# Top-k positions in PSUM, gate products in half steps over three banks, and more row dots inside the gate steps

## The chip, the cores and the metric

The kernel runs on one core of one Trainium2 chip. The metric is the device time of one execution in microseconds; the median of three runs is compared. The engines are called as in the profile: PE (TensorE), DVE (VectorE), ACT (ScalarE), POOL (GpSimd), SP (SyncE, which only issues DMAs here).

## What is computed

The program is a transformer block of two layers for 512 tokens of width 1024. The change touches only the PEER feed-forward of the first layer: each token picks, per head, 16 of 16,384 single-neuron experts.

```
q = (xb @ wq).reshape(PEER_BLOCK, PEER_HEADS, 2, PEER_HALF)
s = einsum('thpd,hpkd->thpk', q, sub_keys)
s_top, i_top = lax.top_k(s, PEER_TOPK)
cand_s = s_top[:, :, 0, :, None] + s_top[:, :, 1, None, :]
cand_i = i_top[:, :, 0, :, None] * PEER_N_KEYS + i_top[:, :, 1, None, :]
best_s, best_pos = lax.top_k(cand_s, PEER_TOPK)
experts = take_along_axis(cand_i, best_pos, axis=-1)
g = softmax(best_s)
act = gelu(einsum('thkd,td->thk', expert_u[experts], xb))
out = einsum('thk,thkd->td', g * act, expert_v[experts])
```

## The kernel before

**Two ways through the experts.** For three of the four blocks of 128 tokens (384 tokens, `TD = 3`) the kernel computes all experts densely: 128 "U tiles" (one tile is 128 experts: 24 matmuls of 384 columns, with each weight split into a high and a low part, `whi` and `wlo`), and later 128 "V tiles". The gates of these tokens are scattered into a dense array by "gate steps". For the last block of 128 tokens each token's own 128 expert rows are fetched instead: an indirect DMA on POOL's queue (`fetch_u`, 128 rows of 4 KB, one for each partition, 512 KB in all) brings one expert row per token into a ring of four buffers `UROW`, and a DVE instruction (`dot`) multiplies it with the token's row and sums. There are 128 such dots. Row k may be fetched once dot k-4 is done.

**The order of the work** is written out by hand, engine by engine, with semaphores between. On DVE it is: the top-k of the scores (`lists_top`), the four `topk` blocks (in the order token block 3, 0, 1, 2; the last three carry 6, 11 and 11 dots between their instructions), 96 gate steps, the tail of the U tiles, and the V tiles.

**U tiles.** For each, SP loads the raw weights, ACT rounds them to `whi` (line 777), POOL (line 641) or, for the last tiles, DVE (line 2301) computes `wlo`, PE multiplies (lines 1275 to 1277), and ACT applies gelu into `actb` (line 982) and stores it. There are four buffers each. 36 tiles run beside the top-k. PE then waits for the normalised gates (`gsel`, line 2247), transposes them, and runs four more tiles.

**Gate steps.** Step q handles four tokens. POOL subtracts indices (`OJ`, shown as T, line 708), DVE makes one-hot matrices `OI` (line 2271) and `OG` (line 2275), PE multiplies them, four matmuls of 256 columns into one pair of PSUM banks (line 1596), ACT copies the high half to `GS` (line 1018), and DVE adds the low half (line 2285). Banks 4 and 5 serve the even steps, 6 and 7 the odd ones. Before each group of four PE does five eighths of a U tile, so 60 tiles (`GATE_TILES`) lie in the 96 steps. Bank 3 holds `window`, the indices and gates of 32 steps. Banks 2 and 3 hold `x_row`, the rows of the last token block, until then; ACT has copied them to SBUF as `sc_row` (shown as rr), and dots from number 28 on read that copy.

**The tail** is the 28 U tiles after the gate steps: PE does nothing else, DVE makes their `wlo` and two dots after each of 25 tiles, and SP stores the last of the dense gates. Then come the **V tiles**, in which DVE makes the products, their low parts, `wlo`, an addition of one fetched V row, and a dot in every tile that `V_DOT_TILES` lists.

In `topk` the found positions `bp` are split into a row and a column (`bab`, then `babf` as float), corrected in a few small instructions, and compared with `iota` to pick the indices.

Of the kernel before, what the change touches and what calls it, by code (L numbers as in the profile page):

```python
# [19 lines left out]
U32 = mybir.dt.uint32  # L20
# [6 lines left out]
P = 128  # L27
# [41 lines left out]
GATE_TILES = 60  # L69
# [42 lines left out]
def build(nc, A, out):  # L112
    with ExitStack() as ctx:
# [111 lines left out]
        bab = a2("bab", [P, 2, NH, 16], U32)  # L225
        babf = a2("babf", [P, 2, NH, 16])
# [410 lines left out]
        def _(pool):  # L637
# [133 lines left out]
        def _(act):  # L771
# [239 lines left out]
            def g_group(q, m, stored=None):  # L1011

                act.wait_ge(g_done, q + 1)
                if stored is not None:
                    act.wait_ge(g_out[m // 16], stored)
                t = 4 * (m % 16)
                high = pair[m % 2][:, :, :].rearrange("p b (t w j) -> p w j (b t)", t=2, w=2)[:, 0]
                nc.scalar.activation(GS[:, m // 16, :, t:t + 4], high, ACT.Copy).then_inc(g_high, 1)

            def gate_blocks(i, first):  # L1020

                for n in range(32):
                    u = 5 * n // 8
                    if n == 0 or 8 * u // 5 == n or -(-8 * u // 5) == n:
                        ahead(G0["U"], u % 4, i * 5 + (GATE_IT + u // 4))
                    if n >= 2:
                        g_group(i * 32 + (n - 2), n - 2, i * 64 if (n - 2) % 16 == 0 and not first else None)
                    elif not first:
                        g_group(i * 32 + (n - 2), n + 30)
                    if 8 * u + 7 < 5 * n + 5:  # L1030
                        it = i * 5 + (GATE_IT + u // 4)
                        act_tile(it * 4 + u % 4, u % 4, it * 32 + 16 * (u % 4 // 2))

            gate_blocks(0, True)
            with act.Fori(1, TD) as i:
                gate_blocks(i, False)
            for m in (30, 31):
                g_group(32 * (TD - 1) + m, m)
# [233 lines left out]
        def _(pe):  # L1272
# [316 lines left out]
            def gate_group(q, half, peeled=False):  # L1589
# [13 lines left out]
            def gate_step(i, n):  # L1603

                for unit in range(5 * n, 5 * n + 5):
# [1138 lines left out]
```

## Time and profile before

| | us |
|---|---|
| median of three runs | 2507.83 (2507.5 to 2508.65) |
| profiled execution, its own time | 2507.04 |
| span of the profiled execution | 2505.2 |
| PE busy | 2414.8 (96% of the span) |
| DVE busy | 1558.9 (62%) |
| POOL busy | 1238.3 (49%) |
| ACT busy | 938.6 (37%) |

The span runs from the first to the last instruction; the execution's own time has 1.84 us more around it. The mean granted clock of PE is 0.991.

### The profile page before, as it was taken

To read this page: it belongs to the slowest core of one execution; us is meant where nothing else is said; L and a number is where in the kernel's file an instruction comes from. 1 tells how busy PE (TensorE), PEld (TensorE's weight loads), DVE (VectorE), ACT (ScalarE), POOL (GpSimd) and SP (SyncE) were. 2 spreads that over 40 slices of the span, in tenths; PEclk is the share of its full clock that TensorE was granted. 3 is DMA by queue.
4 is the path that set the end of the run, shared out by engine and by line. 5 is a ranking of instruction groups with operands and counts; after the bars stand their busy time and mean duration, and the time that the engine had idled before them with its cause. 6 is when DMAs were issued, how large, how long until landed. Compare 5 with 4: busy or idle time off the path is not lost.

```text
span 2505.2 us, 36450 instructions
## 1 busy us (share of the span) xinstructions
PE 2414.8 (96%) x12832; PEld 2165.7 (86%) x12832; DVE 1558.9 (62%) x2682; ACT 938.6 (37%) x1394; POOL 1238.3 (49%) x676
## 2 busy tenths in 40 slices
PE   7999998999889999898999999999999999999998
PEld 4878886899889999888999999998867888888887
DVE  5268333899968888677999899886256414422201
ACT  4473333333434444333333333333344323332222
POOL 3305443348768888554555454544402544444443
PEclk9999999999999999999999999999999999999999
DMA  7228433248856777899999999993301333333332
GB/s 274 75 110 286 154 93 126 85 122 270 281 163 226 246 270 232 333 370 362 394 395 395 389 394 376 392 335 103 100 26 50 116 95 99 87 94 98 101 94 75
DMA packets 254500, 518.83 MB, mean 207 GB/s; under 512 B 117760, under 2 KB 150912, under 8 KB 250048
## 3 DMA queue, kind: packets, MB, share of 16 engines
q1 hardware_dynamic: 197552, 350.01, 42.9%
q0 software_dynamic: 38416, 142.36, 14.6%
q10 hardware_dynamic: 18432, 25.17, 2.7%
q8 instruction: 56, 0.92, 0.2%
q14 instruction: 44, 0.36, 0.0%
HBM read 462.95 MB, written 54.53 MB: 207 GB/s over the span
## 4 chain that ended last, share of the span: by engine, by line
PE 66%; DVE 14%; DMA 12%; issue 4%; SPq 3%; ACT 1%; POOL 1%; ACTq 0%; DVEq 0%; POOLq 0%
PE bank L1275 16%; PE bank L1277 16%; PE bank L1276 16%; DMA GJ<-gate_dram 7%; DMA X<-in_u_rows,which 4%; PE pair L1277 3%; PE pair L1275 3%; PE pair L1276 3%; DVE X L2163 2%; PE pair L1596 2%; DVE YROW L2359 2%; SPq L510 1%; DVE wlo L2301 1%; DVE T L2228 1%; SPq L594 1%
## 5 line engine op out<-in xcount | busy, mean ns | idle before, releaser
L641 POOL TENSOR_TENSOR wlo<-wraw,whi 128x1024 fp32r<-128x1024 f32 x303 | 743.1, 2456 | 802.7 <-ACT whi L777 801.8
L1275 PE MATMUL bank<-HH,whi 128*128 128x512 f32 (+1 forms) x2048 | 752.7, 368 | 36.1 <-DVE wlo L2301 12.1
L1276 PE MATMUL bank<-HL,whi 128*128 128x512 f32 (+1 forms) x2048 | 745.5, 364 | 0.0
L1277 PE MATMUL bank<-HH,wlo 128*128 128x512 f32 (+1 forms) x2048 | 745.2, 364 | 0.0
L777 ACT ACTIVATE whi<-wraw 128x1024 fp32r<-128x1024 f32 x456 | 481.4, 1057 | 519.1 <-PE bank L1277 214.2
L1275 PEld LDWEIGHTS bank<-HH,whi 128*128 128x128 f32 x2048 | 388.0, 189 | 87.4 <-issue 25.2
L1277 PEld LDWEIGHTS bank<-HH,wlo 128*128 128x128 f32 x2048 | 387.3, 189 | 40.5
L1276 PEld LDWEIGHTS bank<-HL,whi 128*128 128x128 f32 x2048 | 388.0, 189 | 39.4 <-issue 0.5
L701 POOL DMA_INDIRECT VROW<-in_w,which x128 | 214.2, 1673 | 255.2 <-DVE YROW L2359 242.3
L694 POOL DMA_INDIRECT X<-in_u_rows,which x128 | 165.5, 1293 | 100.0 <-DVE dots L2163 73.9
L2301 DVE TENSOR_TENSOR wlo<-wraw,whi 128x1024 fp32r<-128x1024 f32 x153 | 186.3, 1218 | 1.3 <-ACT whi L777 1.3
L1275 PE MATMUL bank<-WH,whi 128*128 128x384 f32 x512 | 172.8, 337 | 3.4 <-DVE WL L2334 3.3
L1275 PE MATMUL pair<-WH,whi 128*128 128x384 f32 x512 | 171.6, 335 | 0.0
L1277 PE MATMUL bank<-WH,wlo 128*128 128x384 f32 x512 | 171.3, 335 | 0.0
L1276 PE MATMUL pair<-WL,whi 128*128 128x384 f32 x512 | 171.3, 335 | 0.0
L1276 PE MATMUL bank<-WL,whi 128*128 128x384 f32 x512 | 171.3, 334 | 0.0
L1277 PE MATMUL pair<-WH,wlo 128*128 128x384 f32 x512 | 171.2, 334 | 0.0
L2359 DVE SCALAR_TENSOR_TENSOR YROW<-VROW,wexp,YROW 128x1024 f32<-128x1024 f32 x128 | 166.0, 1297 | 0.2
L1045 ACT ACTIVATE WH<-AJ 128x384 fp32r<-128x384 f32 x128 | 67.1, 524 | 240.7 <-DVE AJ L2328 240.6
L2163 DVE CUSTOM_DVE_ANT_0 X<-X,rr 128x1024 f32<-128x1024 f32 x100 | 131.3, 1314 | 41.6 <-DMA X<-in_u_rows,which 41.6
L2396 DVE TENSOR_TENSOR T<-bank,rr 128x512 f32<-128x512 f32 x60 | 41.3, 690 | 177.1 <-PE bank L1277 176.9
L982 ACT ACTIVATE actb<-bank 128x384 f32<-128x384 f32 x128 | 63.0, 492 | 213.2 <-PE bank L1277 204.6
(409 smaller groups left out, 3737.3 us busy)
## 6 DMA issues: line engine op xcount, KB each, us to landing
wraw<-in_w SPq DMA_DIRECT2D x456, 512.0 KB, 4.2
act_dram<-actb ACTq DMA_DIRECT2D x128, 192.0 KB
gate_dram<-GS SPq DMA_DIRECT2D x24, 1024.0 KB, 8.3
AJ<-act_dram SPq DMA_DIRECT2D x128, 192.0 KB, 7.1
GJ<-gate_dram SPq DMA_DIRECT2D x128, 192.0 KB, 9.0
adaw<-in_ada SPq DMA_DIRECT2D x32, 512.0 KB, 5.6
ada<-in_ada SPq DMA_DIRECT2D x16, 512.0 KB, 14.2
NB<-in_nab POOLq DMA_DIRECT2D x4, 1024.0 KB, 5.7
```

Source lines behind the costliest of these rows:

```text
L641: nc.gpsimd.tensor_tensor(wlo[:, slot, :, :].rearrange("p k c -> p (k c)"), wraw[:, slot, :, :].rearrange("p k c -> p (k c)"), whi[:, slot ...
L694: pool.indirect_dma_start(UROW[:, k % R, :], None, A["u_rows"], bass.IndirectOffsetOnAxis(which[:, 0, k:k + 1], 0)).then_inc(u_row[k % R], 16)
L701: pool.indirect_dma_start(VROW[:, k % R, :], None, A["w"].rearrange("g p c -> (g p) c"), bass.IndirectOffsetOnAxis(which[:, 1, k:k + 1], 0 ...
L777: nc.scalar.activation(whi[:, slot, :, :].rearrange("p k c -> p (k c)"), wraw[:, slot, :, :].rearrange("p k c -> p (k c)"), ACT.Copy).then ...
L982: nc.scalar.activation(actb[:, u % 2, :], bank[u % 2][:, 0:SD], ACT.Gelu_apprx_tanh).then_inc(tile_evac, 1)
L1045: nc.scalar.activation(WH[:, slot, :], AJ[:, slot, :], ACT.Copy).then_inc(pw_hi, 1)
L1275: pe.matmul(out_, ah, bh, start=first, stop=False, **kw)
L1276: pe.matmul(out_, ah, bl, start=False, stop=False, **kw)
L1277: return pe.matmul(out_, al, bh, start=False, stop=last, **kw)
L2163: nc.vector.tensor_tensor_reduce(UROW[:, n % R, :], UROW[:, n % R, :], x_row if n < TOP_DOTS else sc_row, 1.0, 0.0, ALU.mult, ALU.add, dot ...
L2301: nc.vector.tensor_tensor(wlo[:, slot, :, :].rearrange("p k c -> p (k c)"), wraw[:, slot, :, :].rearrange("p k c -> p (k c)"), whi[:, slot ...
L2359: nc.vector.scalar_tensor_tensor(YROW[:, :], VROW[:, u, :], wexp[:, u:u + 1], YROW[:, :], ALU.mult, ALU.add)\
```

## The change

Four things change. (1) `bab`, `babf` and one of the scratch tiles (`wide`) move from SBUF to PSUM banks 6 and 7, and the conversion of the positions becomes two instructions. (2) The gate steps produce, copy and add in half steps of two tokens, over banks 4, 5 and 6 in turn; bank 7 now holds the window, so banks 2 and 3 keep `x_row`. (3) 64 U tiles instead of 60 lie in the gate steps, 16 eighths to three steps, and 24 dots (every fourth step, reading `x_row` from PSUM) instead of 8. (4) 34 dots instead of 54 lie in the tail, now of 24 tiles, of which DVE makes 21 `wlo`; 42 instead of 38 dots lie in the V tiles. The loops over gate steps on PE and ACT are written out.

```diff
-GATE_TILES = 60
+GATE_TILES = 64
-GATE_DOTS = 8
-U_DOTS = 90
-V_DOT_TILES = [j for j in range(P) if j % 5 in (1, 3)][:P - U_DOTS]
-ACTS = (72, 109, P)
+PSUM_DOTS = TOP_DOTS + STEPS // 4
+U_DOTS = 86
+V_DOT_TILES = [j for j in range(P) if j % 16 in (1, 3, 5, 8, 10, 12, 14)][:P - U_DOTS]
+ACTS = (60, 105, P)
...
+        bab = bank[6][:, 256:512].bitcast(U32).rearrange("p (w h k) -> p w h k", w=2, h=NH)
+        babf = bank[7][:, 0:256].rearrange("p (w h k) -> p w h k", w=2, h=NH)
+        wide = bank[7][:, 256:384].rearrange("p (h k) -> p h k", h=NH)
+        gate_window = bank[7]
...
-                if 8 * (lows - gate0 - 3) // 5 + 1 == q:
+                if 3 * (lows - gate0 - 3) // 2 + 1 == q:
                     lo(G0["U"] + lows, lows % R)
                     lows += 1
-                if q >= 16 and q % 12 == 4:
+                if q >= 8 and q % 4 == 0:
                     fetch_u(fetched)
...
+            def gate_group(q):
+
                 pe.wait_ge(og_ready, q + 1)
-                if not peeled:
-                    pe.wait_ge(g_evac, q - 1)
-                for e in range(4):
-                    t = 4 * half + e
-                    mm = pe.matmul(bank[4 + 2 * half + e // 2][:, e % 2 * 256:e % 2 * 256 + 256], OI[:, t, :],
-                                   OG[:, half, :, e, :], start=True, stop=True)
-                mm.then_inc(g_done, 1)
+                for h in (2 * q, 2 * q + 1):
+                    if h >= 3:
+                        pe.wait_ge(g_evac, h - 2)
+                    for t in range(2):
+                        e = 2 * (h % 2) + t
+                        mm = pe.matmul(bank[4 + h % 3][:, t * 256:t * 256 + 256], OI[:, 4 * (q % 2) + e, :],
+                                       OG[:, q % 2, :, e, :], start=True, stop=True)
+                    mm.then_inc(g_done, 1)
...
-                then(nc.vector.tensor_copy(babf[:, :, :, :], bab[:, :, :, :]))
-                row, place, beyond, wide = babf[:, 0, :, :], babf[:, 1, :, :], last[:, 0, :, :], last[:, 1, :, :]
+                place, beyond, row = last[:, 0, :, :], last[:, 1, :, :], babf[:, 0, :, :]
+                nc.vector.tensor_copy(row, bab[:, 0, :, :])
+                then(nc.vector.tensor_copy(place, bab[:, 1, :, :]))
...
             for q in range(STEPS):
                 if q % 32 == 0:
                     window(q // 32)
-                onehots(q)
+                indices_hot(q)
                 if q >= 2:
-                    g_sum(q - 2)
-                if q % 12 == 11:
+                    gate_sum(2 * q - 4)
+                    gate_sum(2 * q - 3)
+                gates_hot(q)
+                if q % 4 == 3:
                     dot()
...
-            for k in range(4):
-                dot()
             v.wait_ge(w_lo, G0["U"] + U_POOL)
+            tail_dots = U_DOTS - PSUM_DOTS
             for t in range(U_POOL, P):
                 lo(G0["U"] + t, t % R)
-                for k in range(2):
-                    if dotted[0] < U_DOTS:
-                        dot()
+                while dotted[0] < PSUM_DOTS + (t - U_POOL + 1) * tail_dots // (P - U_POOL):
+                    dot()
```

**Place 1, a `topk` block on DVE.** `bp`, `gsel`, `last`, `T` and `iota` lie in SBUF; `pair1` is PSUM banks 6 and 7. Before:

```order
L2211 TENSOR_SCALAR bab<-bp 128x128
L2212 TENSOR_SCALAR bab<-bp 128x128
L2213 TENSOR_TENSOR gsel<-bv 128x128
L2216 CAST babf<-bab 128x256
L2218 SCALAR_TENSOR_TENSOR last<-babf 128x128
L2219 TENSOR_SCALAR last<-babf 128x128
L2220 TENSOR_TENSOR last<-last 128x128
L2221 SCALAR_TENSOR_TENSOR babf<-babf,last 128x128
L2222 TENSOR_SCALAR babf<-babf 128x128
L2223 TENSOR_TENSOR babf<-babf,last 128x128
L2228 TENSOR_TENSOR T<-babf,iota 128x2048
```

In the changed kernel, at the same place on DVE:

```order
L2206 TENSOR_SCALAR pair1<-bp 128x128
L2207 TENSOR_SCALAR pair1<-bp 128x128
L2208 TENSOR_TENSOR gsel<-bv 128x128
L2212 CAST pair1<-pair1 128x128
L2213 CAST last<-pair1 128x128
L2214 SCALAR_TENSOR_TENSOR last<-pair1,last 128x128
L2215 TENSOR_SCALAR pair1<-pair1 128x128
L2216 TENSOR_TENSOR pair1<-pair1,last 128x128
L2217 SCALAR_TENSOR_TENSOR pair1<-pair1,last 128x128
L2218 TENSOR_SCALAR pair1<-pair1 128x128
L2219 TENSOR_TENSOR pair1<-last,pair1 128x128
L2224 TENSOR_TENSOR T<-pair1,iota 128x2048
```

Nothing moved but the places of the operands, and one conversion became two; only the instruction that writes `gsel` keeps both inputs in SBUF.

**Place 2, a gate step with a dot on DVE** (`rr` is the SBUF copy of the rows, `bank` in the dot's row is banks 2 and 3). Before:

```order
L2275 SCALAR_TENSOR_TENSOR OG<-T,bank 128x1024
L2285 TENSOR_TENSOR GS<-pair1,GS 128x128x4
L2163 ISA X,dots<-X,rr 128x1024
L2163 ISA dots 128x1
L2271 TENSOR_TENSOR OI<-iota,bank 128x512
```

In the changed kernel:

```order
L2267 TENSOR_TENSOR OI<-iota,pair1 128x512
L2285 TENSOR_TENSOR GS<-pair1,GS 128x128x2
L2285 TENSOR_TENSOR GS<-pair0,GS 128x128x2
L2275 SCALAR_TENSOR_TENSOR OG<-T,pair1 128x1024
L2158 ISA X,dots<-X,bank 128x1024
L2158 ISA dots 128x1
```

The sum stands in two halves, and ahead of `OG` instead of behind it.

**Place 3, the start of the tail on DVE.** Before, after the last sum:

```order
L2285 TENSOR_TENSOR GS<-pair1,GS 128x128x4
L2163 ISA X,dots<-X,rr 128x1024
L2163 ISA dots 128x1
L2163 ISA X,dots<-X,rr 128x1024
L2163 ISA dots 128x1
L2163 ISA X,dots<-X,rr 128x1024
L2163 ISA dots 128x1
L2163 ISA X,dots<-X,rr 128x1024
L2163 ISA dots 128x1
L2301 TENSOR_TENSOR wlo<-wraw,whi 128x1024
```

In the changed kernel:

```order
L2285 TENSOR_TENSOR GS<-pair1,GS 128x128x2
L2303 TENSOR_TENSOR wlo<-wraw,whi 128x1024
L2158 ISA X,dots<-X,rr 128x1024
L2158 ISA dots 128x1
L2303 TENSOR_TENSOR wlo<-wraw,whi 128x1024
L2158 ISA X,dots<-X,rr 128x1024
L2158 ISA dots 128x1
L2158 ISA X,dots<-X,rr 128x1024
L2158 ISA dots 128x1
```

Four dots ahead of the first `wlo` are gone, and a tile is followed by one or two dots.

## Rows read from the trace of the kernel before

**Rows 1.** Waits of PE: place, what for, total us, times, longest.

```profile
PE pair L1582 <- DVE gsel L2247: 17.4, 1, 17.4
PE bank L1275 <- DVE wlo L2301: 12.1, 11, 2.4
PE bank L1275 <- ACT actb L982: 7.1, 2, 6.4
```

**Rows 2.** Windows: us, busy PE, PEld, DVE, ACT, POOL (instructions), PE clock, DMA share, GB/s.

```profile
523.10:677.90 154.80, 151.64 (x866) 151.20 (x865) 152.98 (x452) 66.02 (x83) 114.16 (x61) 0.99 0.76 248
716.80:1011.70 294.90, 294.63 (x1815) 293.60 (x1814) 249.49 (x306) 143.07 (x214) 252.23 (x162) 1.00 0.70 231
1011.70:1157.50 145.80, 126.38 (x673) 121.01 (x672) 102.15 (x149) 44.96 (x60) 78.17 (x59) 0.95 1.00 374
1157.50:1556.00 398.50, 395.14 (x2266) 392.09 (x2265) 353.06 (x472) 144.76 (x190) 200.60 (x127) 1.00 1.06 385
```

**Rows 3.** Timeline of ACT: start, length, the end of two U tiles.

```profile
607.41 0.49 ACT L982 ACTIVATE actb<-bank 128x384 f32<-128x384 f32 x1 [2.13 <-PE bank L1277]
611.57 0.49 ACT L982 ACTIVATE actb<-bank 128x384 f32<-128x384 f32 x1 [2.13 <-PE bank L1277]
```

**Rows 4.** DVE by line, 534.5 to 695.5: count, busy us, mean ns, idle before.

```profile
L2228 DVE TENSOR_TENSOR T<-babf,iota 128x2048 f32<-128x2048 f32 x8 | 20.3, 2541 | 0.2
L2211 DVE TENSOR_SCALAR bab<-bp 128x128 uint32<-128x128 uint32 x4 | 8.8, 2188 | 0.1
L2205 DVE TENSOR_TENSOR T<-T 128x128 f32<-128x128 f32 x4 | 6.6, 1647 | 0.0
L2220 DVE TENSOR_TENSOR last<-last 128x128 f32<-128x128 f32 x4 | 5.4, 1360 | 0.1
L2216 DVE CAST babf<-bab 128x256 f32<-128x256 uint32 x4 | 4.1, 1016 | 0.1
L2213 DVE TENSOR_TENSOR gsel<-bv 128x128 f32<-128x128 f32 x4 | 3.4, 848 | 0.0
L2223 DVE TENSOR_TENSOR babf<-babf,last 128x128 f32<-128x128 f32 x4 | 3.3, 836 | 0.0
```

**Rows 5.** Timeline of DVE in one `topk` block, and of POOL beside it.

```profile
573.94 5.35 DVE L2211 TENSOR_SCALAR bab<-bp 128x128 uint32<-128x128 uint32 x1
...
579.35 0.28 DVE L2213 TENSOR_TENSOR gsel<-bv 128x128 f32<-128x128 f32 x1
579.66 0.29 DVE L2216 CAST babf<-bab 128x256 f32<-128x256 uint32 x1
...
628.85 2.29 DVE L2228 TENSOR_TENSOR T<-babf,iota 128x2048 f32<-128x2048 f32 x1
...
569.84 9.36 POOL L641 TENSOR_TENSOR wlo<-wraw,whi 128x1024 fp32r<-128x1024 f32 x4
```

**Rows 6.** A row fetch on POOL, its dot on DVE, and landing times of rows, 600 to 670.

```profile
655.58 0.95 POOL L694 DMA_INDIRECT X<-in_u_rows,which  x1 [0.16 <-issue]
...
664.28 1.19 DVE L2163 CUSTOM_DVE_ANT_0 X<-X,bank 128x1024 f32<-128x1024 f32 x1
...
DMA to landing us min/median/max: 5.3/6.2/7.3
```

**Rows 7.** Gate steps, 720 to 1011: groups by line.

```profile
L2285 DVE TENSOR_TENSOR GS<-pair,GS 128x512 f32<-128x512 f32 x94 | 64.2, 684 | 3.1 <-ACT GS L1018 3.1
L777 ACT ACTIVATE whi<-wraw 128x1024 fp32r<-128x1024 f32 x59 | 62.7, 1063 | 36.1 <-ACT actb L982 35.0 <-issue 1.1
L1018 ACT ACTIVATE GS<-pair 128x512 f32<-128x512 f32 x94 | 55.4, 590 | 54.6 <-PE pair L1596 54.5
L2163 DVE CUSTOM_DVE_ANT_0 X<-X,rr 128x1024 f32<-128x1024 f32 x8 | 19.1, 2389 | 0.0
```

**Rows 8.** Tail, 1011.7 to 1157.5: the dots by line, and the fetches' median us to landing.

```profile
L2163 DVE CUSTOM_DVE_ANT_0 X<-X,rr 128x1024 f32<-128x1024 f32 x55 | 67.1, 1223 | 41.6 <-DMA X<-in_u_rows,which 41.6
...
X<-in_u_rows,which POOLq DMA_INDIRECT x55, 7.9
```

More of the change, by code:

```diff
@@ L583, in store_g @@
                              GS[:, b % 2, j, :].rearrange("p j t -> p (j t)")).then_inc(g_out[b % 2], 16)
+            stored_at = [-(-32 * (b + 1) // 3) + 6 for b in range(2 * TD)]
             for n in range(GATE_TILES + TAIL):
                 load_w(gu0 + n, (gu0 + n) % R)
-                if n >= 17 and n % 10 in (7, 8, 9, 0) and (n - 17) // 10 < 2 * TD:
-                    store_g((n - 17) // 10, (n - 17) % 10)
+                for b in range(2 * TD):
+                    if 0 <= n - stored_at[b] < 4:
+                        store_g(b, n - stored_at[b])
             def load_ag(j, slot, peeled=False):
@@ L1009, in _, with gate_high @@
                 act_tile(m, u, 16 * (m // 2))
-            def g_group(q, m, stored=None):
-                act.wait_ge(g_done, q + 1)
+            def gate_high(h, stored=None):
+                act.wait_ge(g_done, h + 1)
                 if stored is not None:
[L1015 to L1038, printed above, removed]
+                    act.wait_ge(g_out[h // 32 % 2], stored)
+                t = 2 * (h % 32)
+                high = bank[4 + h % 3].rearrange("p (t w j) -> p w j t", t=2, w=2)[:, 0]
+                nc.scalar.activation(GS[:, h // 32 % 2, :, t:t + 2], high, ACT.Copy).then_inc(g_high, 1)
+            def gate_tile(u):
+                m = 4 * GATE_IT + u
+                act_tile(m, u % 4, 16 * (m // 2))
@@ new lines, in _ @@
+            for n in range(STEPS + 2):
+                v_, part = n // 3, n % 3
+                if part == 0 and n < STEPS:
+                    ahead(G0["U"], 4 * GATE_IT + 2 * v_)
+                for h in range(2 * n - 4, 2 * n - 2):
+                    if h >= 0:
+                        gate_high(h, 64 * (h // 64) if h % 32 == 0 and h >= 64 else None)
+                if part == 1 and n < STEPS:
+                    gate_tile(2 * v_)
+                    ahead(G0["U"], 4 * GATE_IT + 2 * v_ + 1)
+                if part == 2 and n < STEPS:
+                    gate_tile(2 * v_ + 1)
@@ L1587, in _ @@
                 u_tile(G0["U"] + 4 * LEAD_IT + u, u)
[L1589 removed]
+            def gate_group(q):
                 pe.wait_ge(og_ready, q + 1)
[L1592 to L1598 removed]
+                for h in (2 * q, 2 * q + 1):
[6 more added lines that the diff above has]
+                    mm.then_inc(g_done, 1)
             gu0 = G0["U"] + 4 * GATE_IT
             pe.wait_ge(gt_split, 1)
[L1603 to L1605 removed]
+            for n in range(STEPS):
+                for unit in range(16 * n // 3, 16 * (n + 1) // 3):
                     u = unit // 8
[L1607 to L1610 removed]
+                    u_blocks(gu0 + u, u % R, (unit % 8,))
                 if n:
[L1612 to L1617 removed]
+                    gate_group(n - 1)
+            gate_group(STEPS - 1)
             with pe.Fori(0, TAIL // 4) as i:
@@ L2222, in topk @@
                 nc.vector.tensor_scalar(row, row, -1.0, None, ALU.add)
-                then(nc.vector.tensor_tensor(place, place, wide, ALU.add))
+                then(nc.vector.tensor_tensor(babf[:, 1, :, :], place, wide, ALU.add))
                 idx = tkf.rearrange("p (h w) a -> p w h a", w=2)
@@ L2289, in _ @@
                     window(q // 32)
-                onehots(q)
+                indices_hot(q)
                 if q >= 2:
-                    g_sum(q - 2)
-                if q % 12 == 11:
+                    gate_sum(2 * q - 4)
+                    gate_sum(2 * q - 3)
+                gates_hot(q)
+                if q % 4 == 3:
                     dot()
-            for q in range(STEPS - 2, STEPS):
-                g_sum(q)
+            for h in range(2 * STEPS - 4, 2 * STEPS):
+                gate_sum(h)
             def lo(g, slot):
```

41 lines of the change are left out of this document (16 added, 25 removed).

## The prediction

> **What bounds the kernel now.** I read the waits of PE first, since PE is the engine that is busy nearly always, then windows by stage, then the timelines of the engine that PE waits for. In the stages that the change touches PE is idle in two places. It stands 17.4 us before its transposes until DVE has the gates [rows 1]; DVE is busy 153.0 of 154.8 us there [rows 2], so DVE's chain of top-k instructions sets that end. And it waits in the tail, 12.1 us for DVE's `wlo` and 7.1 us for `actb` [rows 1]. A U tile takes 4.16 us (611.57 - 607.41) [rows 3], so 28 need 116.5 us where the tail took 145.8 [rows 2]: 29.3 us are lost. DVE waits there 41.6 us for fetched rows [rows 8] and the DMA share is 1.00 [rows 2]. The gate steps (294.6 of 294.9 us busy) and most of the V stage (395.1 of 398.5) are bound by PE itself [rows 2].
>
> **Top-k: what the move to PSUM removes.** Several small DVE instructions have lengths far over their work. The shift `bab<-bp` took 5.35 us at 573.94; it ended at 579.3, and POOL's run of four `wlo` was 569.84 to 579.20 [rows 5]. The conversion took 0.29 us undisturbed [rows 5] and 1.02 on average [rows 4]. So DVE instructions stand until a POOL instruction lets go. Which ones do is told by the dots: with the row in SBUF, beside the data in SBUF, a dot takes 2.39 us on average [rows 7], with the row in PSUM 1.19 [rows 6].
>
> Excess over undisturbed length for the instructions that lose an SBUF operand [rows 4, 5]: line 2211 8.8 - 4 x 0.22 = 7.9; 2220 5.4 - 4 x 0.28 = 4.3; 2216 4.1 - 4 x 0.29 = 2.9; 2223 3.3 - 1.1 = 2.2; 2228 20.3 - 8 x 2.29 = 2.0. (For the undisturbed shift I take 0.22, a little under the 0.28 of 2213; with 0.28 the sum is 0.2 less.) Sum 19.3 us, on a chain that ends in PE's wait. Two things stop it from all arriving:
> - 2213 (`gsel`, excess 3.4 - 1.1 = 2.3 now) and 2205 (6.6 - 1.1 = 5.5) keep two SBUF inputs. In block two 2213 stands right behind the 5.35 us; with 2211 free it meets the same POOL run. That run begins with the row offsets of block one, which come some 2.4 us earlier (one stand of 2220 and a bit of 2228), so about 2.5 of those 5.1 us are gained, not all. In block four I charge 0.7.
> - The dots inside the blocks need rows, and POOL fetches one after each `wlo`, at the tiles' pace of 4.16 us. Row 21 was fetched at 655.58 and used at 664.28; landing takes 6.2 [rows 6], so it had 2.5 us of slack. POOL itself gets earlier by 2.4 (above) and by some 2 (the 2.3 us comparisons of 2228 no longer hold it), so up to dot 21 the gain is at most about 6.8. What is saved behind dot 21 (2.7 of 2211, 2.9 of 2216, less 0.7) is 4.9 more.
>
> I charge 0.3 us for the extra conversion and slower access in that last part, and less before it, under the cap. Gain 6.8 + 4.9 - 0.3 = 11.4, taken as **11**. Bounds: 3 (nearly every stand passes on to 2213 and 2205) and 17.4 (the whole wait of PE). There is a rule against this edit in the Trainium skill ("VectorE: DVE Perf Modes", Why PSUM operands drop a tier): a PSUM operand costs a float instruction its double rate. By it some six instructions of 128 elements would be about 0.07 us longer in each block, 1.7 us in all, an estimate from that page; the gain would be 10.
>
> **Gate steps: length.** A step now has 16 matmuls of 384 columns instead of 15: 4.16/24 = 0.173 us. 96 steps cost 16.6 us more and the tail has 4 x 4.16 = 16.6 less: zero, if PE stays the bound. Does it? Busy time over 294.9 us now and over 311.5 after:
> - DVE 249.5 [rows 2]. Out: 8 dots, 19.1, and the sums, 64.2 [rows 7]. In: 192 half sums; the length lies between 0.28 (128 elements, rows 5) and 0.684 (512, rows 7), in proportion 0.42 us, so 80; and 24 dots of 1.2 (the one of rows 6 reads PSUM: 1.19), 29. Sum 275, 88%. The dots in gate steps now take 2.39 us on average against 1.2, for both inputs are in SBUF; from PSUM they don't.
> - POOL 252.2 [rows 2] + 4 `wlo` of 2.34 [rows 5] + 15 fetches of 0.95 [rows 6] = 276, 89%.
> - ACT 143.1 + 192 x 0.40 (from 0.59 for 512 elements and 0.49 for 384 [rows 3, 7]) - 55.4 + 8 = 172, 55%.
>
> The order matters more than the shares. The second half of a group waits for a bank that is free when DVE has added the first half of the group before. From the end of a group PE has 15 to 18 matmuls to do, 2.6 us or more. Beside them ACT does, one step in three, `whi` first (1.06), then two halves (0.8), and DVE the one-hot (0.68) and the half sum (0.42): at the worst 2.3 us. After a dot step DVE starts up to 1.2 late, but then `OI` overlaps what ACT does and the sum is there at about 2.5. Hidden, with 0.1 to 1.5 us to spare, where the old order had over 2. I take 0 for the stage. If the cover goes, it is 96 times what is missing.
>
> POOL queues a fetch behind a `wlo` and ahead of the next `OJ`, so each fetch makes an `OJ` 1 us later. POOL runs up to four steps ahead, and has 1 us in 3.2 free on two steps of three: DVE should not see it.
>
> **Tail.** Rows fetched in it fall from 55 to 36 (54 of 90 are fetched before). Megabytes: rows 36 x 0.524 = 18.9; V rows 4 x 0.524 = 2.1; raw weights some 23 x 0.524 = 12.3; `actb` 24 x 0.197 = 4.7; gate stores 4.2; first V operands 1.6: sum 43.8, where before it was 374 GB/s x 145.8 us = 54.5. At 374 GB/s this would be 117 us; the V stage holds 385 over 400 us [rows 2], 114. PE needs 24 x 4.16 = 100. The old 374 was in part set by the ring: four rows in flight and 7.9 us to landing [rows 8] allow one dot in 2.0 us, and with waits it was 145.8/54 = 2.7. DVE now needs 34 dots, at 2.7 92 us, and has 21 tiles (87 us) and the lead that it begins with, up to 3 tiles. So DVE about keeps up, and PE's wait for `wlo` (12.1) nearly goes; the passage to the V stage, where ACT stands for V's weights and PE for `actb` (7.1), I halve. Between 100 and 117 I take 109: 100 + 4 + 5 for the 1 MB stores. Against 145.8 - 16.6 = 129.2 the **tail gives 20** (12 to 27).
>
> **V stage.** Four more dots and rows (2.1 MB). DVE has 353 of 398 us busy; 4 x 1.2 are hidden. The DMA share is 1.06 at 385 GB/s: if that is the ceiling, 2.1/0.385 = 5.5 us come back, if not, 0. PE loses only 3.4 us there now, so I take 1.
>
> **Sum.** -11 + 0 - 20 + 1 = -30 against the profiled execution's span of 2505.2 and own time of 2507.04: span 2475, own time 2477. The median of the runs shown (2507.83) is 0.8 us over that time, so the forecast is **2478**.
>
> **Rivals.**
> - *The stands in the top-k only change place* (chance 0.14): gain 3 instead of 11, 2487. For it: 2213 and 2205 already stand 7.8 us. Against it: POOL is busy 114 of 155 us, so a stand is a matter of chance for each of the eight instructions left. The Trainium skill has this rival as a rule ("SBUF — State Buffer", Who interferes with whom): two inputs in SBUF are enough for a DVE instruction and a GpSimd instruction that reads SBUF to shut each other out for their whole length, and whichever starts first holds. Rows 5 agree, as far as 2211 and POOL's run go.
> - *The tail is bound by its bytes* (0.15): 117 us, gain 12, 2487. For it: share 1.00. Against it: the V stage moves more at 1.06. With the rival above it would be 2495 (0.03 of the two).
> - *The half-step handshake becomes the bound* (0.06): slower. DVE's first half sum would come after PE's 2.6 us. It decides from 30/96 = 0.31 us of waiting a step on; at 0.5 us it is 48, and the result 2508 - 30 + 48 = 2526. For it: the spare time in a dot step is about 0.1 us. Against it: DVE has 12% free to catch up, so the delay doesn't add up.
> - *Nothing comes of it* (0.03): the row fetches hold the top-k at its old pace and bytes the tail, 2508.
> - *As forecast* (0.62): its own range 2470 to 2490.
>
> **Range and chances.** 2478 is the likeliest. The range, 2468 to 2497, holds the forecast with its bounds (-17.4 in the top-k and -27 in the tail, both at once, would give 2465) and both middle rivals, also together. A difference under 0.2% (5 us) can't be told from none. Faster 0.90, same 0.03, slower 0.07.
>
> **What would show it.** Top-k: the PSUM instructions at 0.2 to 0.3 us, the wait for `gsel` near 6 to 9 us, and new waits of DVE for rows inside the blocks. Gate steps: 311 us, PE without idle time, dots at 1.2 us each. Tail: near 109 us, wait for `wlo` under 4 us. V stage: as long as before, its GB/s a little over 385. Wrong it would be by a step of over 3.3 us in the gate steps, by a tail at 117, or by 2213 taking over the 5 us stand in every block.

## The result, and the profile after

The changed kernel takes 2479.98 us (median of four runs, 2478.29 to 2481.64), the kernel before on the same chip 2508.24 (2507.5 to 2509.91). The ratio is 0.9892 (0.9880 to 0.9904): 28 us faster. The forecast was 2478. The profiled execution after took 2481.35 us, its span is 2479.5.

The span falls by 25.7 us. I split it at four events that both traces have: the start of PE's transposes of the gates, the start of its last gate matmul, the end of the U tiles and the end of the V tiles. Four tiles moved from the tail into the gate steps, so in the last column 4 x 4.16 = 16.6 us are taken off the gate steps and added to the tail.

| event or stretch | before | after | difference, tiles set off |
|---|---|---|---|
| transposes start | 695.53 | 684.65 | -10.9 |
| to the last gate matmul | 315.8 | 337.7 | +5.3 |
| to the end of U | 146.1 | 105.0 | -24.5 |
| V tiles | 542.0 | 544.7 | +2.7 |
| rest, second layer | 805.7 | 807.5 | +1.8 |

The waits of PE after, from 480 to 1700 us (what it waited for; us in total, times, longest), to be set against [rows 1]:

```profile
PE pair L1584 <- DVE gsel L2243: 9.9, 1, 9.9
PE bank L1277 <- DVE WL L2334: 4.8, 9, 1.1
PE bank L1277 <- ACT actb L986: 2.9, 1, 2.9
PE pair L1599 <- DVE GS L2285: 2.0, 2, 1.2
```

The wait for `gsel` fell from 17.4, the one for `wlo` in the tail (12.1) is gone, the one for `actb` fell from 7.1. New are two waits for half sums.

The windows after (length, busy PE, PEld, DVE, ACT, POOL, then clock, DMA share, GB/s): gate steps, tail, and the first 399 us of V, against the last three of [rows 2].

```profile
706.80:1022.40 315.60, 312.81 (x1908) 310.75 (x1907) 268.67 (x436) 161.49 (x318) 271.45 (x183) 1.00 0.73 251
1022.40:1127.30 104.90, 102.01 (x579) 101.63 (x579) 72.96 (x104) 38.09 (x51) 49.80 (x39) 0.98 1.03 400
1127.30:1526.00 398.70, 393.96 (x2255) 390.02 (x2254) 354.39 (x475) 144.53 (x190) 200.66 (x130) 1.00 1.06 387
```

The tail now moves 400 GB/s where it moved 374, so 374 was no ceiling.

**Top-k.** DVE in the second block after, and POOL beside it:

```profile
572.10 0.29 DVE L2206 TENSOR_SCALAR pair<-bp 128x128 uint32<-128x128 uint32 x1
572.30 0.28 DVE L2207 TENSOR_SCALAR pair<-bp 128x128 uint32<-128x128 uint32 x1
572.50 7.44 DVE L2208 TENSOR_TENSOR gsel<-bv 128x128 f32<-128x128 f32 x1
579.97 0.30 DVE L2212 CAST pair<-pair 128x128 f32<-128x128 uint32 x1
...
567.99 11.78 POOL L645 TENSOR_TENSOR wlo<-wraw,whi 128x1024 fp32r<-128x1024 f32 x5
```

The shift that stood 5.35 us [rows 5] takes 0.29: its input is still in SBUF, its output is in PSUM. Two instructions later `gsel`, whose inputs and output lie in SBUF, stands for 7.44 us, until POOL's run of five `wlo` ends at 579.8. It stands for another 2.3 us in the next block. Over the whole top-k, the lines of DVE that had the stands, 534 to 684, against [rows 4]:

```profile
L2224 DVE TENSOR_TENSOR T<-pair,iota 128x2048 f32<-128x2048 f32 x8 | 18.3, 2289 | 0.2
L2208 DVE TENSOR_TENSOR gsel<-bv 128x128 f32<-128x128 f32 x4 | 10.3, 2580 | 0.0
L2201 DVE TENSOR_TENSOR T<-T 128x448 f32<-128x448 f32 x4 | 4.7, 1169 | 0.0
L2200 DVE TENSOR_TENSOR T<-T 128x128 f32<-128x128 f32 x4 | 4.1, 1027 | 0.0
L2218 DVE TENSOR_SCALAR pair<-pair 128x128 f32<-128x128 f32 x4 | 1.2, 300 | 0.1
L2206 DVE TENSOR_SCALAR pair<-bp 128x128 uint32<-128x128 uint32 x4 | 1.2, 291 | 0.1
```

The excess over undisturbed lengths was 27.1 us before: the 19.3 of the prediction's sum, 2.3 of `gsel` and 5.5 of the first candidate sum. It is 9.2 (`gsel`) + 2.3 and 3.0 (the two candidate sums, L2201 and L2200) = 14.5 now, all in lines that keep two inputs in SBUF. That is 12.6 less. The ten small instructions with an operand in PSUM cost some of it back (11.6 us in all, where the nine before would take 9.4 undisturbed): 10.9 arrive.

**Gate steps.** PE around the last gate group (start, length):

```profile
1020.10 0.87 PE L1599 MATMUL pair<-OG,OI 128*128 128x256 f32 x6
1022.15 0.51 PE L1599 MATMUL pair<-OG,OI 128*128 128x256 f32 x2 [1.18 <-DVE GS L2285]
```

and DVE and ACT beside it:

```profile
1018.76 1.23 DVE L2275 SCALAR_TENSOR_TENSOR OG<-T,pair 128x1024 fp32r<-128x1024 f32 x1
1019.89 1.23 DVE L2158 CUSTOM_DVE_ANT_0 X<-X,bank 128x1024 f32<-128x1024 f32 x1
1021.03 0.10 DVE L2158 DVE_READ_ACCUMULATOR2_ANT dots<- 128x1 f32 x1
1021.62 0.81 DVE L2285 TENSOR_TENSOR GS<-pair,GS 128x256 f32<-128x256 f32 x2 [0.49 <-ACT GS L1022]
...
1021.20 0.97 ACT L1022 ACTIVATE GS<-pair 128x256 f32<-128x256 f32 x3 [0.41 <-PE pair L1599]
```

The last group has no U matmuls in front of it. Its last half needs a bank that ACT copies at 1021.20 and DVE adds at 1021.62, and PE stands for 1.2 us. In the steps before, U matmuls lie over that chain.

**Tail.** DVE's dots there, against [rows 8]:

```profile
L2158 DVE CUSTOM_DVE_ANT_0 X<-X,rr 128x1024 f32<-128x1024 f32 x34 | 41.5, 1224 | 18.7 <-DMA X<-in_u_rows,which 17.2 <-issue 1.4
```

They still wait for rows, 17.2 us instead of 41.6, but no `wlo` comes late by it. What the DMA queues moved in the tail (1022.4 to 1127.3):

```profile
DMA packets 16309, 41.97 MB, mean 400 GB/s; under 512 B 4599, under 2 KB 8075, under 8 KB 15796
```

ACT at the passage to V, where the first `whi` of V waits for its raw weights and `actb` stands behind it:

```profile
1119.38 1.06 ACT L781 ACTIVATE whi<-wraw 128x1024 fp32r<-128x1024 f32 x1 [8.70 <-DMA wraw<-in_w]
1120.34 0.51 ACT L1047 ACTIVATE WH<-AJ 128x384 fp32r<-128x384 f32 x1
1120.75 0.47 ACT L986 ACTIVATE actb<-bank 128x384 f32<-128x384 f32 x1
```

### The profile page after: what moved, and what is told of

It is laid out like the page before. It is cut to its first block, busy times and chain, and to the rows that moved or that the text cites. A ratio compares the mean times of both kernels' runs of the same rounds, so it can differ in the third digit from the quotient of the medians.

```text
span 2479.5 us, 36308 instructions
## 1 busy us (share of the span) xinstructions
PE 2411.5 (97%) x12832; PEld 2163.5 (87%) x12832; DVE 1541.1 (62%) x2778; ACT 951.2 (38%) x1490; POOL 1220.5 (49%) x680
## 3 DMA queue, kind: packets, MB, share of 16 engines
q1 hardware_dynamic: 197552, 350.01, 41.6%
## 4 chain that ended last, share of the span: by engine, by line
PE 64%; DVE 16%; DMA 10%; issue 5%; SPq 3%; ACT 2%; POOL 0%; ACTq 0%; DVEq 0%; POOLq 0%
PE bank L1277 16%; PE bank L1279 16%; PE bank L1278 16%; DMA GJ<-gate_dram 7%; PE pair L1279 3%; PE pair L1278 3%; PE pair L1277 3%; DVE X L2158 3%; DMA X<-in_u_rows,which 2%; DVE YROW L2359 2%; SPq L512 2%; PE pair L1599 2%; DVE wlo L2303 1%; SPq L598 1%; DVE WL L2334 1%
## 5 line engine op out<-in xcount | busy, mean ns | idle before, releaser
L705 POOL DMA_INDIRECT VROW<-in_w,which x128 | 206.8, 1616 | 260.6 <-DVE YROW L2359 242.8
L698 POOL DMA_INDIRECT X<-in_u_rows,which x128 | 156.1, 1219 | 78.6 <-DVE dots L2158 51.7
L2275 DVE SCALAR_TENSOR_TENSOR OG<-T,pair 128x1024 fp32r<-128x1024 f32 x96 | 116.8, 1217 | 15.7 <-POOL T L712 15.7
```

Of the source, the lines that this page charges most:

```text
L698: pool.indirect_dma_start(UROW[:, k % R, :], None, A["u_rows"], bass.IndirectOffsetOnAxis(which[:, 0, k:k + 1], 0)).then_inc(u_row[k % R], 16)
L705: pool.indirect_dma_start(VROW[:, k % R, :], None, A["w"].rearrange("g p c -> (g p) c"), bass.IndirectOffsetOnAxis(which[:, 1, k:k + 1], 0 ...
L2275: nc.vector.scalar_tensor_tensor(OG[:, q % 2, :, :, :].rearrange("p w t j -> p w (t j)"), bc(oj, 1, 2), 0.0, bc(gate_window[:, P + 8 * n:P ...
```

## The experiments

Four questions stood open: whether the top-k's gain is what the move to PSUM does; what caps it; whether the rows are what held the tail; and what the half steps bring. Each expectation sets theories against each other, called A and B (or more), and the text behind it says which held. All times are medians; "before" was run on the same chip each time (2506.50 to 2507.54). The stretches are split as in the table above, each as a difference to the kernel before with moved tiles set off; they come from one trace for each kernel.

**1 and 2. The scratch in PSUM, taken back and alone.**

```diff
 e1, on the changed kernel:
-        bab = bank[6][:, 256:512].bitcast(U32)...
-        babf = bank[7][:, 0:256]...
-        wide = bank[7][:, 256:384]...
+        bab = a2("bab", [P, 2, NH, 16], U32)
+        babf = a2("babf", [P, 2, NH, 16])
+        wide = a2("wide", [P, NH, 16])
 e2, on the kernel before: the reverse
```

> The changed kernel (2480) with the top-k scratch tiles back in SBUF, all else kept. Theory A (the stands of DVE behind POOL are what the PSUM placement removed): about 10 us of the gain come back, 2490 (2487 to 2494), PE's wait for the gates near 17 to 20 us, single small instructions of 2 to 5 us in the top-k blocks. Theory B (the top-k's end moved for another reason, as the row fetches or the first block): 2480 to 2483.

> The kernel before with only the top-k scratch tiles in PSUM, nothing else changed. Theory A: 10 to 11 us faster than before, 2497 to 2499, all of it in PE's wait for the gates (17.4 to about 7); gate steps 295 and tail 146 as they were. Theory B (it needs the other edits, or the tail takes it back, since it is bound by DMA): no change or under 3 us.

e1: 2490.73 us, ratio 0.9935 (0.9914 to 0.9955). Transposes at 695.60, PE's wait for `gsel` 17.6; 5.36 us at 573.86 stand again on a shift. e2: 2495.33, ratio 0.9963 (0.9945 to 0.9981). Transposes at 684.00 (-11.5); behind them the gate steps and the V stage are as before, the tail is 2.3 us shorter and the last stretch 1.7 longer. Theory A holds in both; e2 is 1.7 us faster than its range. Taken back or alone, the part is worth 11 to 12 us.

**3. The stand on `gsel`.** A copy of the best scores in PSUM, so that the subtraction has one input there:

```diff
+        highest = bank[7][:, 384:392]
...
+                nc.vector.tensor_copy(highest, bv[:, :, 0])
...
-                nc.vector.tensor_tensor(gsel[...], bv[:, :, :], bc(bv[:, :, 0], 2, 16), ...
+                nc.vector.tensor_tensor(gsel[...], bv[:, :, :], bc(highest, 2, 16), ...
```

> The changed kernel, and the last small instruction of that group with two inputs in SBUF (the one that writes the gates' differences, which stood 7.4 and 2.3 us) reads one of them from PSUM after a copy of 8 columns. Theory A (stands vanish with the second SBUF input, but the dots' rows come at the tiles' pace): 9.7 us of stands go, but dots 15, 16 and 21 had only 1.6 to 2.3 us over a landing time of 6.2, so 2 to 4 us arrive, 2476 to 2478, and DVE waits for rows inside the blocks. Theory C (the chain is DVE's alone): 9 us, 2471. Theory D (the stand passes on to the next instruction with two SBUF inputs): 2479 to 2481.

2479.09 us, ratio 0.9887. The 9.2 us of stands on `gsel` are gone, and so are the 2.3 on L2201; the transposes are only 2.7 us earlier (681.95), for now DVE waits inside the blocks:

```profile
DVE X L2159 <- DMA X<-in_u_rows,which: 7.1, 7, 1.6
```

That is theory A's mechanism: the supply of rows, one fetch for each tile's `wlo`, does cap the top-k; in the changed kernel it was not reached. The V stage took 1.6 us more than in the changed kernel, and the time moved by 1, less than A's 2 to 4 and inside the scatter.

**4. The gate dots from SBUF in the half steps.**

```diff
-x_row if n < PSUM_DOTS else sc_row
+x_row if n < TOP_DOTS else sc_row
```

> The changed kernel with the 24 dots of the gate steps reading the SBUF copy of the row instead of PSUM. Theory A (a dot with two SBUF inputs stands for POOL, 2.4 us on average, and the half sums leave PE about 0.3 us to spare in a dot step): gate steps 325 to 345 us instead of 316, total 2490 to 2508. Rival (DVE has 12 per cent free and the delay is absorbed): gate steps under 319, total within 3 us of 2480.

2481.93 us, ratio 0.9901. The dots took 1.31 us, not 2.4. Groups by line on DVE and POOL in the gate steps (709 to 1023) of this run:

```profile
L2158 DVE CUSTOM_DVE_ANT_0 X<-X,rr 128x1024 f32<-128x1024 f32 x24 | 31.5, 1314 | 0.0
L645 POOL TENSOR_TENSOR wlo<-wraw,whi 128x1024 fp32r<-128x1024 f32 x64 | 158.5, 2476 | 24.1 <-ACT whi L781 23.6
L698 POOL DMA_INDIRECT X<-in_u_rows,which x23 | 28.4, 1234 | 3.4 <-issue 1.1
```

POOL's two groups in the changed kernel, same stretch:

```profile
L645 POOL TENSOR_TENSOR wlo<-wraw,whi 128x1024 fp32r<-128x1024 f32 x64 | 154.3, 2410 | 40.1 <-ACT whi L781 40.1
L698 POOL DMA_INDIRECT X<-in_u_rows,which x24 | 22.8, 951 | 3.7 <-issue 0.9 <-DVE dots L2158 0.2
```

Here mostly POOL stands, 4 us on `wlo` and 6 on the fetches, and takes it out of its own idle time. PE waits 3.9 us for half sums instead of 2.0, and the steps are 1.2 us longer. The rival holds: whether the dots read PSUM or SBUF makes 2 us in the time, inside the scatter.

**5. The dots moved, and nothing else.** On the kernel before: whole steps, two pairs of banks, 60 tiles, SBUF rows.

```diff
-                if q >= 16 and q % 12 == 4:
+                if q >= 8 and q % 4 == 0:
...
-                if q % 12 == 11:
+                if q % 4 == 3:
...
-            for k in range(4):
-                dot()
...
-                for k in range(2):
-                    if dotted[0] < U_DOTS:
-                        dot()
+                while dotted[0] < 52 + (t - U_POOL + 1) * (U_DOTS - 52) // (P - U_POOL):
+                    dot()
```

> The kernel before with one thing changed: 24 dots (every fourth step) instead of 8 lie in its whole gate steps, reading the SBUF copy of the rows, the four dots ahead of the tail are gone, and 38 dots are spread over 25 tail tiles. Top-k, whole steps over two pairs of banks, 60 tiles in the steps and the V stage stay. It asks whether the half steps and the row in PSUM were needed for the dots to move. Theory A (the tail is held by its row fetches; any place outside the tail will do for the dots): 41 rows instead of 55 in the tail, 28 tiles need 116.5 us, the tail goes from 146 to 120 to 126, PE's wait for wlo from 12 to under 3, the gate steps stay at 295 to 297: the span is 18 to 26 us less, the time about 2484 (2480 to 2489). Theory B (whole steps with dots from SBUF, up to 2.4 us each, stretch the steps: DVE has then 250 + 16 x 1.2 to 2.4 of 295 us and a step's OG comes late): PE waits for one-hots or sums in the gate steps, 8 to 20 us longer, and the time is 2492 to 2503.

2481.25 us (2478.88 to 2486.70), ratio 0.9890 (0.9874 to 0.9907): 9 us faster than the whole change without its top-k part (experiment 1), and the two intervals are apart. The tail fell by 24.8 us, to 121.4 for 28 tiles. In the steps the dots do stand, and so do POOL's fetches:

```profile
L2163 DVE CUSTOM_DVE_ANT_0 X<-X,rr 128x1024 f32<-128x1024 f32 x23 | 53.4, 2324 | 0.0
L694 POOL DMA_INDIRECT X<-in_u_rows,which x22 | 37.1, 1687 | 3.3 <-issue 1.7
```

and PE hardly sees it: it waits 0.2 us for `GS`, and the steps are 2.0 us longer. Theory A holds.

**6. No row fetches in the tail.**

```diff
+UNFETCHED = range(40, 94)
...
+                if k in UNFETCHED:
+                    return
```

The dots of these 54 rows read `sc_row` in place of the fetched row, so the kernel leaves their expert activations out of its result.

> The kernel before without the fetches of rows 40 to 93 (their dots read the SBUF copy of the tokens' rows in place of the fetched row, so those expert activations are left out of the result; the number and length of DVE's instructions stay). It asks what the row fetches alone cost the tail. Theory A (rows, by their landing and their bytes, hold the tail): the tail goes from 146 to 117 to 123 us, PE waits for wlo under 2 us and little for actb, the time is 2479 to 2484, and tail's DMA share falls under 0.8. Theory B (DVE's work order, two dots after each wlo, or the passage to the V stage holds it): wlo waits stay over 6 us or actb's 7, the tail stays over 130 us, the time is over 2491.

2476.12 us, ratio 0.9873. The same dots on DVE, none waiting, and the tail takes 116.8 us where 28 tiles need 116.5; the DMA share is 0.71. Both of PE's waits, for `wlo` and for `actb`, are gone. Theory A, and beyond its range, since the V stage is 3.1 us shorter too. The row fetches were all of the tail's loss of 29 us, the passage to V included. They bring both their time to landing and their bytes; no run takes one away without the other, so how the loss divides between the two stays open.

**7. A cover for the last gate group.**

```diff
+            u_tile(gu0 + GATE_TILES, 0)
             gate_group(STEPS - 1)
...
```

The loop of tail tiles then begins with the second.

> The changed kernel with the last gate group put behind the first tail U tile on PE, so that its two half sums have matmuls in front of them. Theory A (the half steps' chain PE, ACT, DVE, PE must be covered by U matmuls; where it isn't, PE stands): the gap of 2.05 us at the last group goes, the tail and the V stage begin that much earlier, the time is 1 to 2.5 us less than the changed kernel's, 2477.5 to 2479. Theory B (the tail is bound by its bytes, so time won ahead of it isn't kept): the tail gets as much longer, the time is within 0.5 us of the changed kernel's.

2481.51 us, ratio 0.9898. The wait of 1.2 us at the last group is gone, and PE's wait for `actb` at the end of the tail is 4.7 us in place of 2.9. Nothing reached the end. That is theory B's effect, though the wait is at the passage to V, not spread over the tail, and the time (1.5 us over the changed kernel's) is inside the scatter.

**8. Four dots back from V to the tail.**

```diff
-U_DOTS = 86
+U_DOTS = 90
```

> The changed kernel with 38 dots in the tail and 38 in the V stage instead of 34 and 42. It asks how the tail and the V stage share the four dots. Theory A (the tail still has room, the V stage is at its ceiling of about 385 GB/s): the V stage is 2 to 3 us shorter (398.7 to 396), the tail up to 1 us longer than 106.9, the time 1 to 2 us less than the changed kernel's. Theory B (the tail at 400 GB/s is bound by its bytes): 2.1 MB more cost it 3 to 6 us, DVE's dots come late, wlo waits return, and the time is 1 to 4 us more than the changed kernel's.

2483.09 us (2478.67 to 2486.21), ratio 0.9905. In the trace the V stage is 2.5 us shorter (542.2) than in the changed kernel and the tail 3.2 longer, most of it in PE's wait for `actb` (5.1): both theories in part, and no difference in the time that is clear of the scatter. Four dots with their rows cost the V stage 2.5 us.

**9. Two parts alone.** Experiment 2 with experiment 5: scratch in PSUM and dots in the whole steps. No half steps, no third bank, no row in PSUM, 60 tiles.

> The kernel before with two parts of the change alone: the top-k scratch in PSUM, and 24 dots from the SBUF copy in its whole gate steps with the rest of the dots spread over 25 tail tiles. No half steps, no third bank, no row in PSUM, still 60 tiles in the steps, 38 dots in the tail and 38 in the V stage. It asks whether the half steps earn anything. Theory A (they cost: 3 us of waits for half sums in the gate steps, and 42 dots instead of 38 cost the V stage 2.6 to 4; the two parts alone add up, 12 + 26 us): transposes at 684 to 685, gate steps 293 to 297, tail 120 to 123, V stage 540 to 543, the time 2469 to 2475, 5 to 11 us less than the changed kernel. Theory B (the gains don't add, for with an earlier gate stage the rows and the stores meet elsewhere; the half steps pay for the row in PSUM and the 64 tiles): 2478 to 2484, no better than the changed kernel.

2469.72 us (2468.24 to 2471.46), ratio 0.9854 (0.9837 to 0.9870). The interval lies below that of the changed kernel, which is 10 us slower. The windows of gate steps and tail:

```profile
708.90:1002.60 293.70, 293.01 (x1798) 290.51 (x1797) 276.68 (x335) 142.59 (x213) 276.58 (x177) 1.00 0.77 256
1002.60:1119.30 116.70, 116.70 (x675) 116.70 (x675) 83.48 (x117) 45.21 (x60) 56.97 (x44) 1.00 1.03 397
```

Theory A holds, and PE is busy for the whole tail. ACT's first `whi` of V waits 2.3 us there:

```profile
1109.60 1.06 ACT L778 ACTIVATE whi<-wraw 128x1024 fp32r<-128x1024 f32 x1 [2.25 <-DMA wraw<-in_w]
```

Against the changed kernel, moved tiles set off, the stretch to the last gate matmul is 3.0 us shorter, the tail 4.9, V 3.3. The difference of the spans is 11.5.

**10. Both stands gone, in the changed kernel.** Experiment 3, and a copy of one half of the candidate sums' operands:

```diff
+                then(nc.vector.tensor_copy(wide, halves[:, 0]))
...
-                one, two = halves[:, 0], halves[:, 1]
+                one, two = wide, halves[:, 1]
```

> The changed kernel with the two small DVE instructions that still stand in its top-k given a PSUM operand too: the best score that gsel subtracts (a copy of 8 columns more) and one half of the candidate sums (a copy of 128 columns more). Theory A (behind the stands comes the supply of rows, one fetch for each tile's wlo): transposes at 681 to 683, no more than with gsel alone (681.95), DVE's waits for rows inside the blocks rise from 7.1 to 9 to 11 us; the time within 1.5 us of 2479. Theory B (rows have slack): transposes at 678 to 680, PE's wait for gsel 3 to 6 us, the time 2475 to 2477.

2476.66 us (2472.09 to 2477.61), ratio 0.9882 (0.9866 to 0.9899). Transposes at 680.53, 1.4 us earlier than in experiment 3 and between the two theories' ranges; DVE waits 8.8 us for rows, near A's 9 to 11; the time is in B's range, but its interval overlaps that of the changed kernel. So the cap by the rows shows, and what it is worth in time does not. The tail lost its wait for `actb`, the V stage (546.1) got one of 2.9 us. DVE there:

```profile
1133.27 0.56 DVE L2331 TENSOR_TENSOR AJ<-AJ,GJ 128x384 f32<-128x384 f32 x1 [7.89 <-DMA GJ<-gate_dram]
...
1137.23 0.55 DVE L2337 TENSOR_TENSOR WL<-AJ,WH 128x384 fp32r<-128x384 f32 x1
```

I read this as the same lateness of V's first transfers, seen one wait further on.

**11. Rows sooner.** The same with the cover of experiment 7, and twice the fetches of the late top-k:

```diff
-                if t > 25 and fetched < R + TOP_DOTS and t % 4 == 0:
+                if t > 17 and fetched < R + TOP_DOTS and t % 2 == 0:
```

> The same, with a second row fetch in every other tile from tile 18 on (instead of every fourth from tile 26 on), and the last gate group behind the first tail tile. Theory A (the rows are what holds the top-k when the stands are gone): DVE's waits for rows in the blocks fall under 3 us, transposes at 673 to 678, PE's wait for gsel under 4 us, the gate stage begins 6 to 10 us earlier than in the changed kernel; if the tail and the V stage keep their lengths, the time is 2472 to 2476. Theory B (what comes earlier is given back: POOL's wlo of the tiles beside the top-k come later by the fetches, or the tail and the V stage are longer): PE waits for POOL's wlo there, 3 us or more, or U's end is no more than 2 us earlier, and the time is 2477 or more.

2483.27 us, ratio 0.9907. DVE's waits for rows fell to 1.6 us, and DVE was through its last block 7 us earlier than in experiment 10 (671.75 against 678.69). But the fetches delay POOL's `wlo`, PE waits 4.3 us for them, and the 36th tile ends at 679.9 instead of 672.9. ACT has its last exponential of the gates behind that tile, and DVE stands for it:

```profile
679.93 0.49 ACT L987 ACTIVATE actb<-bank 128x384 f32<-128x384 f32 x1 [2.24 <-PE bank L1280]
...
682.12 0.31 ACT L1001 ACTIVATE gsel<-gsel 128x128 f32<-128x128 f32 x1
682.53 0.69 DVE L2247 TENSOR_REDUCE hs<-gsel 128x32 f32<-128x512 f32 x1 [10.77 <-ACT gsel L1001]
...
683.63 2.70 DVE L2249 TENSOR_TENSOR gsel<-gsel,hs 128x512 f32<-128x512 f32 x1
```

The last multiplication, two inputs in SBUF, takes 2.70 us where it takes 0.69 in the changed kernel, beside POOL's `wlo` again. The transposes start at 686.39. Theory B. So behind the rows lies a second bound, the order on ACT: in experiment 10 that exponential ended at 675.4, 3.3 us before DVE came for it, so with the tiles at that pace no supply of rows could have given more than 3.3.

**12. The same stands in the kernel with two parts.** Experiment 10's copies on experiment 9's kernel.

> The kernel with the two parts alone (top-k scratch in PSUM, 24 dots in the whole gate steps, 2469.7 us), and the operands of gsel and of the candidate sums from PSUM as well. It asks whether what the stands give reaches the end of a program whose tail and V stage have room. Theory A (it does: its tail took 117.2 us where 28 tiles need 116.5, so nothing behind gives time back): transposes at 680 to 682, 3 to 4 us earlier than 684.45, DVE's waits for rows in the blocks 8 to 10 us, and the time 3 to 4 us less, 2465.5 to 2467.5. Theory B (as in the changed kernel, where 2.7 us less in the top-k came with 1.6 us more in the V stage and 1 us in the time): the V stage rises from 541.4 to 543 or more, and the time is 2468.5 or more.

2466.85 us (2464.66 to 2468.34), ratio 0.9840 (0.9827 to 0.9854): the fastest. Transposes at 681.41, 3.0 us earlier than in experiment 9; the tail stays at 116.8 and V at 540.3, which is theory A. The time is 2.9 us less than experiment 9's. The two intervals overlap, so the time alone does not show it; the traces, which differ by 3.0 at the transposes and by no loss behind them, agree with it.

The traces side by side, as differences to the kernel before:

| | transposes | gate | tail | V | rest | span |
|---|---|---|---|---|---|---|
| changed | -10.9 | +5.3 | -24.5 | +2.7 | +1.8 | -25.7 |
| 4, SBUF dots | -11.1 | +6.5 | -23.9 | +2.4 | +0.2 | -25.8 |
| 5, dots only | +0.5 | +2.0 | -24.8 | -1.0 | +3.0 | -20.3 |
| 6, no tail rows | +0.1 | +0.2 | -29.4 | -3.1 | +0.8 | -31.5 |
| 9, two parts | -11.1 | +2.3 | -29.4 | -0.6 | +1.6 | -37.2 |
| 12, and no stands | -14.1 | +2.8 | -29.4 | -1.7 | -0.1 | -42.4 |

(The last stretch, which no edit touches, scatters by 3 us. Experiment 5's span says 20 and its median 26: its profiled execution took 2486.70 us, the slowest of its four, and the last stretch holds some of that.)

## Why the prediction was right, and where it was not

- **Top-k, -11:** -10.9, and experiments 1 and 2 give 10.9 and 11.5 at the transposes. The sum arrived, but not by the road described. The cap by the rows, which I let decide up to dot 21, was not reached: no DVE wait for rows in the blocks. What held the gain was `gsel`, of which I had said that "about 2.5 of those 5.1 us are gained": it stood 7.44 us at that place, 2 longer than the shift had, since DVE came there 1.4 us earlier and POOL's run, now of five `wlo`, ended 0.6 us later. PE's wait for `gsel` stayed at 9.9, above the forecast of 6 to 9. Two errors cancelled, so the size of this term was right by luck. The rival in which the stands "only change place" described what happened at this place, but not what became of the other stands. Experiment 3 showed that the cap exists, 11.5 us of stands removed for 2.7 us.
- **The price of PSUM:** the small instructions take 0.28 to 0.30, as forecast, but the price was under-charged: 2.2 us over the four blocks (11.6 against 9.4), half of it the extra conversion, where the sum had 0.3. The Trainium skill's page "SBUF — State Buffer" (Who interferes with whom) says that only DVE instructions that need the port shared with GpSimd are shut out. Rows agree: with an operand in PSUM none of eleven instructions stood, with all of them in SBUF `gsel` did for 7.44 us. The shift L2211, by which the prediction bore out its rule of two inputs, has only one, with its output in SBUF too; of two inputs it shows nothing, `gsel` does.
- **Gate steps, 0:** +5.3, failed in size. The step was "Hidden, with 0.1 to 1.5 us to spare", worked out for a group with U matmuls ahead of it. The last group has none, and PE waits 1.2 us there; behind the third window's copies of indices and gates another 0.8 was missing. From the first to the last gate matmul it is 291.5 us before and 312.6 - 16.6 = 296.0 after, 4.5 more; experiments 5 and 9 have 1.8 of that with whole steps and 24 dots, so the half steps are some 3, of which the waits are 2.0. The rival of a bound handshake stayed false.
- **"From PSUM they don't" (the 2.4 us dots):** SBUF dots stand in the old order (2.32 in experiment 5), but in the half steps they take 1.31 (experiment 4). Neither cost PE much: 0.2 us of waits in the one, 1.9 more in the other.
- **Tail, -20:** -24.5. The direction and mechanism hold (experiments 5, 6). Mis-sized was the rate: I counted 43.8 MB and took a middle between 117 us, that at 374 GB/s, and PE's 100 us. 42.0 MB moved at 400, and the waits for `wlo` vanished entirely.
- **V stage, +1:** +2.7. It is the four dots and rows (experiment 8: 2.5 back); "hidden" was wrong for `WL`, for which PE waits 4.8 us instead of 3.3.
- **The sum, -30:** 28 in the medians, 25.7 in the traces. The tail gave 4.5 us more than its term, the gate steps took 5.3 and the V stage 1.7 more than theirs: here too errors cancelled. In the rivals, 2487 and 2495 are each 1 us above what their own terms give.
- **What the prediction didn't ask:** what each part is worth. Parts 2 to 4 of the change read as one construction. But 16 more dots in the old gate steps and an even spread in the tail give all of the tail's gain and more. The half steps, the row in PSUM, the 64 tiles and the dots sent to V cost 10 us together (experiment 9): 3.0 in the gate steps, 4.9 in the tail and its passage to V, 3.3 in V. Why the passage stands is shown in part. ACT waits 8.7 us for V's first raw weights in the changed kernel, 2.3 in experiment 9; both tails run near 400 GB/s, but one has 12 us more for the same stores, first V operands and a few rows more. That it is this length that counts I argue and have not tried: no run has 64 tiles with whole steps, or 60 with half steps.

## What to carry to other kernels

When an instruction of one engine stands behind another's, an operand in PSUM can free it, but the next one in line that keeps all of its operands in SBUF can take the stand, as `gsel` did. Count those before booking the gain, and look for the supply, and for the other engine's order of work, that cap the rest. And when a change is a bundle, price each part against the kernel before: the simple part, moving row fetches from a stage whose transfers are full to one with 0.70 of share, was worth 26 us by itself where the whole bundle gave 28, and the machinery built for it took 10 away.

## What was not expected of the hardware

- **A stand lasts over a whole run, not one instruction.** `gsel`, 0.28 us of work, stood 7.44 us until the end of POOL's five back-to-back `wlo`. These took 11.78/5 = 2.36 us each, as they do elsewhere (2.41 on average in the gate steps), so POOL lost nothing.
- **Who stands is a matter of phase.** In the whole steps of experiment 9 a dot that starts beside POOL's subtraction of indices, and the fetch that starts 0.7 us behind the dot, are both long:

```profile
727.93 1.05 POOL L709 TENSOR_TENSOR T<-iota,T 128x512 f32<-128x512 f32 x1
...
728.43 1.63 DVE L2164 CUSTOM_DVE_ANT_0 X<-X,rr 128x1024 f32<-128x1024 f32 x1
...
729.12 1.76 POOL L695 DMA_INDIRECT X<-in_u_rows,which  x1
```

  In experiment 4 the dots, also from SBUF, took 1.31 us on average, and POOL paid.
- **A stop of PE costs more than its length.** After the 2.9 us wait for `actb` (its end at 1121.4) the granted clock is full for another 1.2 us or a little more, then falls to the lower level:

```profile
1118.20:1121.30 3.10, 0.27 (x2) 0.00 (x0) 0.83 (x1) 1.85 (x3) 2.49 (x3) 1.00 1.02 419
1121.50:1122.60 1.10, 1.10 (x7) 1.10 (x8) 0.69 (x2) 0.90 (x1) 0.00 (x0) 1.00 1.02 417
1122.60:1126.00 3.40, 3.40 (x13) 3.40 (x12) 2.58 (x3) 2.42 (x5) 0.00 (x0) 0.54 1.03 419
```

  In 3.4 us PE does 13 matmuls, where at the full clock 8.0 us hold 48, so 20: seven matmuls, 1.2 us. In experiment 9, without the wait, the same passage runs at 1.00 throughout.
